# HGRN2: the next head's dense groups between the levels of this head's recurrence

## What is computed

```python
xn = rms_norm(h, norm_g)
q, f_logit, i, g = jnp.split(xn @ w_in, 4, axis=-1)
f = lb + (1.0 - lb) * jax.nn.sigmoid(f_logit)
q, k, v, log_f = silu(q), 1 - f, i, log(f)      # 8 heads of 128
...
# one chunk: S_t = diag(f_t) S_{t-1} + k_t v_t^T, o_t = S_t^T q_t
b = jnp.cumsum(log_f, axis=2)
decay = exp(b_t - b_s) for t >= s, else 0
scores = jnp.einsum('bhtk,bhtsk,bhsk->bhts', q, decay, k)
o = scores @ v + (q * exp(b)) @ S
...
o = rms_norm(o, o_gain) * jax.nn.sigmoid(g)
h = h + o @ w_out
```

## Time and profile before

| | |
|---|---|
| time, three runs | median 3078.87 us, 3076.29 to 3081.34 |
| profiled execution | 3075.35 us, its span 3073.6 us |
| mean granted TensorE clock | 0.969 of 2.4 GHz |
| ACT's high part of a unit, 128x1024 | 1.04 to 1.06 us |
| masks: transfer of 2.1 MB, cast on DVE | issued 864.8, landed 8.2 us later; 2.30 us |
| busy share PE, PEld, DVE, ACT, POOL | 96%, 83%, 48%, 35%, 7% |

### The profile page before, as it was taken

The page is one execution under the profiler, slowest core; times in us unless marked ns, Lnnn a source line. Parts: engine busy times, 40 slices in busy tenths (PEclk is TensorE's granted clock), DMA queues, the critical chain, the costliest instruction groups (busy, mean ns, idle before and its releaser), DMA issues.

```text
span 3073.6 us, 46468 instructions
## 1 busy us (share of the span) xinstructions
PE 2937.2 (96%) x17931; PEld 2548.8 (83%) x17931; DVE 1462.0 (48%) x2048; ACT 1089.2 (35%) x1717; POOL 206.7 (7%) x169
## 2 busy tenths in 40 slices
PE   8999999999999867799999999999999999799998
PEld 7877779999999866699988888887788887588887
DVE  5555545554344566555553444543533334544432
ACT  4333334333243443343332232332344444332222
POOL 1000000000000122210000110110100000200000
PEclk9999989999999877799999999999999999899999
DMA  4221213332343200033333323223211112233332
GB/s 124 52 61 49 61 42 95 90 89 83 95 121 89 61 1 0 0 90 95 89 92 94 104 69 93 78 71 89 83 49 48 48 48 73 65 96 94 90 94 71
DMA packets 419424, 225.54 MB, mean 73 GB/s; under 512 B 7461, under 2 KB 416294, under 8 KB 419222
## 3 DMA queue, kind: packets, MB, share of 16 engines
q1 hardware_dynamic: 416310, 211.45, 23.8%
q0 software_dynamic: 2256, 10.32, 1.1%
q10 hardware_dynamic: 784, 2.75, 0.3%
HBM read 222.36 MB, written 2.13 MB: 73 GB/s over the span
## 4 chain that ended last, share of the span: by engine, by line
PE 90%; DVE 5%; issue 2%; ACT 1%; POOL 1%; DVEq 0%; DMA 0%; ACTq 0%; POOLq 0%
PE ps L432 39%; PE ps L428 33%; PE ps L733 2%; PE ps L944 2%; PE ps L825 2%; PE ps L902 1%; PE ps L965 1%; PE ps L933 1%; PE ps L651 1%; PE ps L735 1%; PE ps L745 1%; PE ps L869 1%; PE ps L838 1%; PE ps L849 1%; PE ps L716 1%
## 5 line engine op out<-in xcount | busy, mean ns | idle before, releaser
L400 DVE TENSOR_TENSOR wl<-raw,wh 128x1024 fp32r<-128x1024 f32 (+2 forms) x421 | 512.9, 1218 | 437.6 <-ACT wh L396 434.1
L396 ACT ACTIVATE wh<-raw 128x1024 fp32r<-128x1024 f32 (+2 forms) x421 | 425.7, 1011 | 758.9 <-PE ps L428 395.4
L432 PE MATMUL ps<-xh,wh 128*128 128x264 f32 x2736 | 565.0, 288 | 7.3 <-DVE xl L461 5.5
L432 PE MATMUL ps<-xl,wh 128*128 128x264 f32 x2736 | 559.0, 286 | 0.0
L432 PE MATMUL ps<-xh,wl 128*128 128x264 f32 x2736 | 558.6, 286 | 0.0
L432 PEld LDWEIGHTS ps<-xh,wh 128*128 128x128 f32 x2736 | 428.5, 189 | 15.6 <-issue 4.1
L432 PEld LDWEIGHTS ps<-xl,wh 128*128 128x128 f32 x2736 | 426.1, 189 | 0.0
L432 PEld LDWEIGHTS ps<-xh,wl 128*128 128x128 f32 x2736 | 425.1, 189 | 0.0
L428 PE MATMUL ps<-xh,wh 128*128 128x512 f32 x976 | 392.3, 402 | 17.7 <-DVE xl L461 13.9
L428 PE MATMUL ps<-xl,wh 128*128 128x512 f32 x976 | 388.6, 398 | 0.0
L428 PE MATMUL ps<-xh,wl 128*128 128x512 f32 x976 | 386.4, 396 | 0.0
(11 more groups left out here) (295 smaller groups left out, 3915.7 us busy)
## 6 DMA issues: line engine op xcount, KB each, us to landing
raw<-in_w_in SPq DMA_DIRECT2D x88, 512.0 KB, 3.8
raw<-in_ffn_w_gate SPq DMA_DIRECT2D x44, 512.0 KB, 3.9
raw<-in_ffn_w_up SPq DMA_DIRECT2D x44, 512.0 KB, 3.8
raw<-in_w_ffn_in SPq DMA_DIRECT2D x44, 512.0 KB, 3.8
raw<-in_fox_w_in SPq DMA_DIRECT2D x33, 512.0 KB, 4.2
raw<-in_hgrn_w_in SPq DMA_DIRECT2D x32, 512.0 KB, 4.0
raw<-in_ffn_w_down SPq DMA_DIRECT2D x32, 448.0 KB, 3.5
raw<-in_ffn_w_down SPq DMA_DIRECT2D x16, 512.0 KB, 3.7
```

Of the source, the lines that this page charges most:

```text
L396: nc.scalar.activation(wh[:, v % 2, 0:nk, :], raw[:, v % RAW_SLOTS, 0:nk, :], ACT.Copy).then_inc(s("w_hi"), 1)
L400: nc.vector.tensor_tensor(wl[:, v % 2, 0:nk, :], raw[:, v % RAW_SLOTS, 0:nk, :], wh[:, v % 2, 0:nk, :].bitcast(F32), ALU.subtract).then_in ...
L432: last = nc.tensor.matmul(ps[:, bank + b, 0:HALF], w[:, slot, kk, :], x[:, k, b * HALF:(b + 1) * HALF], start=first, stop=end_)
```

## The change

The three stages become one loop. `PH_HGP` makes f, q, v of head 0 ahead of it. Turn i of the loop (`PH_HG`) has the recurrence of head i and, in halves of four weight tiles (`part`), the groups f, q, v of head i + 1 and the gate of head i. All of them use banks 0 and 1 (`HG_BANKS`), so a group waits for the evacuation of the one before. The levels alternate between banks 2 and 3, the diagonal goes first (`hgrn_level_mm(i, 0)`), the last 16 tokens have a place of their own in bank 6 (`pick_last`), and a pick covers only the columns that its mask can hold. The output sum of a head is made in the next turn. The last head's turn (`PH_HGL`) has the gate and eight early groups of the output projection, over the first 6 of 8 heads; `PH_HGOUT` does the last 2 for each of eight groups. The sigmoids are made of abs, exp and ln (`below`, `sigmoid_log`, `sigmoid`), whose three passes wait for one another, and f, q and the gate lie in six work rows in place of `heads`. POOL makes the distances of all seven levels, those of level 0 a turn ahead. The distances, exponentials and products have three buffers in place of two. The raw gate (group 3, `o_x`) is evacuated at the end of the turn, once `sigmoid_log` has read the buffer. The masks are cast ahead of the loop, beside the first stage. What `hgrn_stage` holds: k, the sigmoid's logarithm for q, the scan, and q times its sigmoid. Some setup semaphores are shared, and two increments that nobody waits for are gone, outside this layer.

```diff
-PH_HGRN = Phase(PH_DOWN0, HG_H, K8)
-PH_HGOUT = Phase(PH_HGRN, 2, K8)
+HG_BANKS = (0, 0)
+HG_EARLY = HG_H - 2
+PH_HGP = Phase(PH_DOWN0, 1, [[KT]] * 3, HG_BANKS)
+PH_HG = Phase(PH_HGP, HG_H - 1, K8, HG_BANKS)
+PH_HGL = Phase(PH_HG, 1, [[KT]] + [[HG_EARLY]] * KT, HG_BANKS)
+PH_HGOUT = Phase(PH_HGL, 2, [[KT - HG_EARLY]] * 4, (0, 2) if (PH_HGL.g0 + PH_HGL.gpi) % 2 else (2, 0))
...
-    def pe_group(pe, ph, i, gj, hi, lo, ready=None):
+    def pe_group(pe, ph, i, gj, hi, lo, ready=None, k0=0, part=None):
...
-        pe.wait_ge(s("psum_free"), ph.g0 + gj + 1 + single + ph.gpi * i)
+        if part != 1:
+            pe.wait_ge(s("psum_free"), ph.g0 + gj + 1 + single + ph.gpi * i)
         uj = sum(map(len, ph.groups[:gj]))
...
             for kk in range(nk):
+                if part is not None and kk // (nk // 2) != part:
+                    k += 1
+                    continue
                 if ready:
                     pe.wait_ge(s(ready[0]), ready[1] + k + 1)
                 for n, (w, x) in enumerate(((wh, hi), (wh, lo), (wl, hi))):
                     first, end_ = k == 0 and n == 0, k == n_k - 1 and n == 2
...
+        for gj in range(3):
+            pe_group(pe, PH_HGP, 0, gj, xh, xl, ("x_ready", KT * 2) if gj == 0 else None)
+            if gj == 0:
+                pe_sum(pe, 2)
...
+        def hgrn(i, last=False):
+            def half(gj, part):
+                if not last:
+                    pe_group(pe, PH_HG, i, gj, xh, xl, part=part)
+                elif gj + part == 0:
+                    pe_group(pe, PH_HGL, 0, 0, xh, xl)
+                else:
+                    early(2 * gj + part - 1)
+            def early(m):
+                if m == 0:
+                    pe.wait_ge(s("y_ready"), KT + HG_EARLY)
+                pe_group(pe, PH_HGL, 0, 1 + m, yh, yl)
+            hgrn_level_mm(i, 0)
+            hgrn_level_mm(i, 1)
+            half(0, 0)
+            hgrn_last_tokens(i)
+            if not first(i):
+                hgrn_out(i - 1)
+            half(0, 1)
+            hgrn_level_mm(i, 2)
+            hgrn_level_mm(i, 3)
+            half(1, 0)
+            half(1, 1)
+            hgrn_level_mm(i, 4)
+            hgrn_level_mm(i, 5)
+            if not first(i):
+                hgrn_sum(i - 1, True)
+            half(2, 0)
+            hgrn_off(i)
+            half(2, 1)
+            hgrn_level_mm(i, 6)
+            hgrn_level_mm(i, 7)
+            half(3, 0)
+            if not last:
+                pe.wait_ge(s("psum_free"), evacuated(PH_HG, i, 2))
+                pe.wait_ge(s("g_off_ready"), i + 1)
+                hgrn_turn(i + 1)
+            half(3, 1)
+            if last:
+                hgrn_out(i)
+                early(KT - 1)
+                hgrn_sum(i, False)
+        pe.wait_ge(s("psum_free"), evacuated(PH_HGP, 0, 2))
+        pe.wait_ge(s("rstd_ready"), 3)
+        hgrn_turn(0)
         hgrn(0)
-        loop(pe, HG_H, hgrn, 1)
-        hgrn_sum(HG_H - 1)
-        dense(PH_HGOUT, yh, yl, ("y_ready", KT))
+        loop(pe, HG_H - 1, hgrn, 1)
+        hgrn(HG_H - 1, True)
+        for i in range(2):
+            for gj in range(4):
+                pe_group(pe, PH_HGOUT, i, gj, yh, yl, ("y_ready", KT + HG_EARLY) if i + gj == 0 else None, HG_EARLY)
         feed_forward(1, PH_UP1, PH_DOWN1, 3, 3)
...
+        def below(x, e, name, n):
+            nc.scalar.activation(e[:, :], x[:, :], ACT.Abs).then_inc(s(name), 1)
+            act.wait_ge(s(name), 3 * n + 1)
+            nc.scalar.activation(e[:, :], e[:, :], ACT.Exp, scale=-1.0).then_inc(s(name), 1)
+            act.wait_ge(s(name), 3 * n + 2)
+            nc.scalar.activation(e[:, :], e[:, :], ACT.Ln, bias=one).then_inc(s(name), 1)
+        def sigmoid(e, n, logs, done):
+            act.wait_ge(s(logs), n + 1)
+            nc.scalar.activation(e[:, :], e[:, :], ACT.Exp).then_inc(s(done), 1)
+        def forget_log(n):
+            act.wait_ge(s("f_done"), n + 1)
+            nc.scalar.activation(f_e[:, :], f_x[:, :], ACT.Ln).then_inc(s("f_log"), 1)
...
+        def hgrn(i, last=False):
+            ph, n = (PH_HGL, 0) if last else (PH_HG, i)
+            def split(uj):
+                split_ahead(act, act_hi, ph, n, uj)
+            hgrn_exp(i, 1)
+            hgrn_exp(i, 2)
+            split(0)
+            if not first(i):
+                hgrn_square(i - 1)
+            act.wait_ge(s("g_vt_mm"), i + 1)
+            copy(g_vt[:, 0:NFULL, :], ps[:, 4, :].rearrange("p (j n) -> p j n", j=NFULL))
+            copy(g_vt[0:TAIL, NFULL, :], ps[0:TAIL, 5, 0:P]).then_inc(s("g_vt_ready"), 1)
+            if not last:
+                act.wait_ge(s("psum_free"), evacuated(ph, n, 0))
+                below(f_x, f_e, "f_below", i + 1)
+            else:
+                split(1)
+            hgrn_exp(i, 3)
+            hgrn_exp(i, 4)
+            if not last:
+                split(1)
+                sigmoid(f_e, i + 1, "f_logs", "f_sig")
+                forget_log(i + 1)
+            else:
+                split(2)
+            if not first(i):
+                sigmoid(o_e, i - 1, "o_logs", "o_sig")
                 hgrn_rsqrt(i - 1)
+            if not last:
+                act.wait_ge(s("psum_free"), evacuated(ph, n, 1))
+                below(q_x, q_e, "q_below", i + 1)
+            else:
+                split(3)
+            hgrn_exp(i, 5)
+            hgrn_exp(i, 6)
+            if last:
+                split(4)
             act.wait_ge(s("g_off_mm"), i + 1)
-            for c0, c1 in ((P, 512), (STRIP_B + P, STRIP_B + 3 * P), (STRIP_C + P, tail_at(4))):
-                last = copy(g_off[:, c0:c1], flat[:, 2048 + c0:2048 + c1])
-            last.then_inc(s("g_off_ready"), 1)
-            if not isinstance(i, int):
+            copy(g_off[:, 0:512], flat[:, 2048:2560])
+            copy(g_off[:, 512:N_HG_OFF], flat[:, 2560:2048 + N_HG_OFF]).then_inc(s("g_off_ready"), 1)
+            if not last:
+                split(2)
+                sigmoid(q_e, i + 1, "q_logs", "q_sig")
+            else:
+                split(5)
+            if not first(i):
                 hgrn_hi(i - 1)
+            if not last:
+                split(3)
+                hgrn_exp(i + 1, 0)
+                hgrn_exps(i + 1)
+                act.wait_ge(s("psum_free"), evacuated(ph, n, 3))
+                below(o_x, o_e, "o_below", i)
+                return
+            below(o_x, o_e, "o_below", i)
+            split(6)
+            sigmoid(o_e, i, "o_logs", "o_sig")
+            split(7)
+            hgrn_square(i)
+            split(8)
+            hgrn_rsqrt(i)
+            hgrn_hi(i)
         hgrn(0)
-        loop(act, HG_H, hgrn, 1)
-        hgrn_square(HG_H - 1)
-        hgrn_rsqrt(HG_H - 1)
-        hgrn_hi(HG_H - 1)
+        loop(act, HG_H - 1, hgrn, 1)
+        hgrn(HG_H - 1, True)
...
+        def hgrn_distance(i, n):
+            width, cols_ = hgrn_level(n)
+            if n == 0:
+                pool.wait_ge(s("g_b_ready"), i + 1)
+            if n >= 3 or not first(i):
+                pool.wait_ge(s("g_e_ready"), HG_LEVELS * i + n - (1 if n else 6))
+            b = hgrn_halves(g_b[:, 0:cols_], n)
+            nc.gpsimd.tensor_tensor(hgrn_halves(g_d[:, hgrn_buffer(n), 0:cols_], n), b,
+                                    b[:, :, width - 1:width].to_broadcast([P, cols_ // (2 * width), 2 * width]),
+                                    ALU.subtract).then_inc(s("g_d_ready"), 1)
+        def hgrn(i, last=False):
             for n in range(1, HG_LEVELS):
-                if n == 1:
-                    pool.wait_ge(s("g_b_staged"), 2 * i + 2)
-                else:
-                    pool.wait_ge(s("g_e_ready"), HG_LEVELS * i + n - 1)
-                hgrn_distance(nc.gpsimd, n).then_inc(s("g_d_ready"), 1)
-        loop(pool, HG_H, hgrn)
+                hgrn_distance(i, n)
+            if not last:
+                hgrn_distance(i + 1, 0)
+        hgrn_distance(0, 0)
...
+        def sigmoid_log(x, e, out, n, below, done):
+            dve.wait_ge(s(below), 3 * n + 3)
+            V.scalar_tensor_tensor(out[:, :], x[:, :], 0.0, e[:, :], ALU.min, ALU.subtract).then_inc(s(done), 1)
+        def forget(n):
+            dve.wait_ge(s("f_sig"), n + 1)
+            carry(dve, "dve_carry")
+            V.tensor_scalar(f_x[:, :], f_e[:, :], col(span, n), col(floor, n), ALU.mult, ALU.add).then_inc(s("f_done"), 1)
+        def hgrn_stage(n):
+            dve.wait_ge(s("f_done"), n + 1)
+            if not first(n):
+                dve.wait_ge(s("g_dt_mm"), n)
+                dve.wait_ge(s("g_lv_mm"), (HG_LEVELS + 1) * n - 7)
+                dve.wait_ge(s("g_qk_ready"), HG_LEVELS * n)
+                dve.wait_ge(s("g_left_ready"), n)
+            V.tensor_scalar(g_k[:, :], f_x[:, :], -1.0, 1.0, ALU.mult, ALU.add)
+            sigmoid_log(q_x, q_e, q_e, n, "q_below", "q_logs")
+            dve.wait_ge(s("masks_loaded"), 32)
+            dve.wait_ge(s("f_log"), n + 1)
+            if not first(n):
```

(119 more changed lines are left out.)

386 lines of the change are left out of this document (178 added, 208 removed).

## The result

The changed kernel takes 3051.01 us (median of 4 runs, 3049.43 to 3051.60) against 3078.63 (median of 4, 3076.29 to 3081.34): a ratio of 0.9909, 95% interval 0.9892 to 0.9926, or 27.6 us less. The forecast was 3081, no change that can be told. The time lies in the stated range, near its lower end, at the turn length that rival (a) gave most of its chance; but it moved down by 0.9%, where the forecast had a small rise. The profiled execution took 3051.09, span 3049.4.

What follows compares the result with a forecast made beforehand. TensorE, busy 96%, was taken as the bound. Turns of 50.3 us (39.7 work, 6.7 holes, 4 lowered clock), last head and output ended at 1353.4 against 1350.55: +3 on the 3078.87 median, rounded down to 3081; range 3048 to 3104.

Steps and rivals of the forecast that it cites:

- rival (a): Loop: TensorE stays the bound, the walked waits being too strict; 3056 us at 47 a turn, 3029 at 43; chance 0.33.
- E: Zero point of each walked turn, the end of `scaled_out(0)`; the first was put at 901.2.
- the wrap: Rest of a turn after `scaled_out(2)`, with TensorE as the chain again: 20.4 us.
- The size of the turn: One loop turn: 50.3 us, from 39.7 of work, 6.7 of holes and 4 of lowered clock.
- the clock behind the second hole: After TensorE's 1.1 us wait for `scaled_out(1)` at group 2: a lowered clock might put `scaled_out(2)` at 30.8, not 29.1.
- the first hole: TensorE waits 2.2 us at level 4 for VectorE's products; some 3.5 us at 1.2 GHz follow, worth 1.7.
- The third hole: TensorE waits 3.4 us for `scaled_out(2)` at group 3, the largest; half the group then takes 4.5 us at lowered clock.
- POOL's port: POOL holds VectorE's two-input operations: `split(1)` 1.69 us for 1.23, a product 1.35 for 0.42; `g_q`'s possible 1.4 left out.
- Last head: From the last head's start to the last y: 37.5 us of turn, then 81.6 for gate and early groups, ending at 1322.1.
- Output: Eight output groups: adds 4.15 us apart, bound by xh, xl and POOL's sum, 29 first to last, ending at 1353.4.
- Rival (b): Loop: slower by lowered clock behind each hole and one more product held by POOL; 53.2 us a turn, 3098; chance 0.22.
- (c): The chain as walked: 49 to 52 us a turn, 3073 to 3093 in total, likeliest 3081; chance 0.45.

Runs made afterwards that it cites:

- left_plus: The changed kernel with four more 128-column products on VectorE in `hgrn_left`, into a tile nobody reads: 3061.97 us.
- wide_picks: The changed kernel with the picks of all products over all 512 columns again: 3058.40 us.
- before_pool_short: The kernel before the change, with POOL's distances of the odd levels taken of the first 128 columns alone: 3075.13 us in one run.
- split1_late: The changed kernel with `split(1)` issued behind products 3 and 4 instead of first in the turn: 3041.82 us.
- early4: The changed kernel with early output groups over 4 heads in place of 6, leaving 4 in place of 2 for the output groups: 3044.96 us.
- pool_short: The changed kernel with POOL's distances formed for the first 128 columns only, the rest left out: 3045.90 us.
- q_first: The changed kernel with `scaled_out(1)`, the evacuation of q, moved ahead of the f logarithm, `hgrn_left` and `forget`: 3054.22 us.

## Why the prediction was wrong

By its own steps, with the end of the last add, 27 us earlier than forecast (1326.37 against 1353.4), as the sum:

- **Bound, floor, ahead of the loop: right.** First E at 901.16 (901.2), work of a turn 40.0 (39.7), the prologue's hole 5.0 (5.6). No table load stands in the loop.
- **The order of the holes: right.** Three a turn, at level 4, at group 2 and at group 3, each released by the instruction named; the wrap from `scaled_out(2)` to E is 20.6 in the usual turn (20.4). left_plus and wide_picks showed that VectorE's list sets the turn up to `scaled_out(1)`. So the time came out at rival (a)'s number, but not by its mechanism: the order of waits was not too strict.
- **The size of the turn: the step that failed.** 279.2 us for six turns where 301.8 was forecast, 22.6 of the 27. Some 20 of them lie between E and `scaled_out(2)`, 2 in the wrap. Two terms were mis-sized. First, VectorE's instructions: `hgrn_left` at 3.5 measured 2.5, since the row of 3.5 was itself lengthened by POOL, as before_pool_short showed for 0.65 of it; and `split(1)` ended at E + 6.0 and not 6.7, as POOL's two distances were over earlier. They make most of the 1.9 us by which `scaled_out(1)` was early, some 12 over six turns. Second, the clock behind the second hole: `scaled_out(2)` was put at E + 29.1, "or E + 30.8 when the hole of 1.1 has cost the clock too", and the turn of 50.3 took the middle. In the usual turn that hole, 1.5 us long, kept 2.4 GHz, and `scaled_out(2)` ended at E + 26.6. That is some 5 over six turns; in which instruction the other 3 or 4 lie was not separated.
- **The clock, further.** As a sum the turn had 4 us of lowered clock, and 1.5 were measured. The prediction took over from the earlier trace rows that a hole of 1.2 us is enough for 1.2 GHz behind it; but the first hole, 1.4 where 2.2 was forecast, lowered it once in six. What it put behind the first hole (1.7) did not lengthen its turn, for there VectorE ended after TensorE, at E + 15.0 against 14.0; the sixth turn and wide_picks bear that out. The third hole's 1.6 came as forecast, 1.5, in five turns of six.
- **POOL's port.** The row at 997.42 and split1_late show the hold as forecast: the instruction held is whichever of VectorE's stands there. By the rule of the Trainium skill (SBUF — State Buffer, "SBUF: two separate sides") the lock goes to the instruction that starts first. The trace agrees: `g_q`, for which the prediction put 1.4 us a turn beside its sum, started 0.26 ahead of POOL and ran in 0.68 us, so it was not held, as the walk had it.
- **Last head: 114.3 from E(6) to the last y where 119.1 was forecast, 4.8 of the 27.** The hole ahead of early 3 is 3.8 (4.1) and has the cause named; the one ahead of early 0 is 3.0 (3.2), the one ahead of early 2 only 1.6 (2.9). In which of the forecast's terms the rest of the 4.8 lies was not separated.
- **Output: right in the sum.** Adds 4.15 apart on the mean (4.15), first to last 29.1 (29). The chain named is there, with 4.0 where POOL holds the split of two tiles; that 3.4 and twice 4.8 beside it bring the mean to the forecast's figure is luck.
- **Chances.** The range held, by the share that it gave to rival (a)'s lengths; the chain's own range, 3073 to 3093, did not. Both mis-sized terms erred towards slow: the first came from a row that POOL had lengthened, the second from one hole, where the changed kernel shows both outcomes for holes alike. Rival (b), slower by the clock and the port, did not come. By its own terms the range runs from 3050 to 3105 and (c) ends at 3091; neither changes what is said here.

What stays open: beside 3048.5 the time of each version fell less than its section, or rose more, by 1 to 7 us (early4: 11.0 and 3.5). Some 2.5 of that may lie in the reference, for the changed kernel's own median is 3051.01, taken when the kernel before had 3078.63; beside it the two differ by -1 to 5. Up to 5 lie behind the last add, where nothing was changed; their cause was not found.

## What to carry to other kernels

Before a duration is carried into a new order, look for what ran beside it on an engine that can hold it up, here POOL: take the shortest row of that shape and add the hold where the new order has one. A hole costs its length only where its end sets the next thing, and a lowered clock only where TensorE is the chain: here a slower TensorE behind the first hole was absorbed by the second. Compare turns in the same state of the clock before a small difference of means is put down to an edit (pool_short). When TensorE waits for evacuations, move the last of them in VectorE's list first; moving one whose reader is not ready gives nothing (q_first), and a moved hold lands on its neighbour (split1_late).

## What the runs showed of the hardware

- Equal holes did not always do the same to the clock. In turns two to seven of the changed kernel the first hole of 1.4 us left 2.4 GHz in place five times and was followed by 1.2 GHz once; the third of 2.7 was followed by it five times and not in the fifth turn, which was 1.5 us shorter for that. In pool_short the clock fell behind the same 2.7 us in three of the loop's five such turns, and in wide_picks it did not fall behind one of 1.9 and one of 2.7 in the second turn. What decides was not found.
- POOL's hold costs POOL much less than VectorE: a distance took 1.05 us in the changed kernel beside `split(1)` and 1.27 in split1_late with two products held, while a held VectorE product goes from 0.43 to 1.30.
